# RWKV opening of a fused 1-core kernel: input loaded first, squares on two engines, key projection ahead of the low-rank products, and those in column and row groups of the array

## The chip, the cores and the metric

The kernel runs on one core of a Trainium2 chip. The metric is the device time of one launch in microseconds, lower is better. Three runs of the kernel before gave 1181.09, 1178.21 and 1175.55 us; the median is 1178.21.

## The reference, cut to what matters

Input x is 256 tokens by 1024 features, all in float32. Two blocks run one after the other: a RWKV-7 layer and a block-sparse attention layer, then an mLSTM layer and a latent-attention layer, each of these with a squared-ReLU MLP and scaled by vectors from a conditioning vector c ("ada"). The change is in the opening of the RWKV layer:

```python
h = rms_norm(x, norm_a)                     # x * rsqrt(mean(x*x) + 1e-6) * g
xx = pad(h, one step)[:, :-1] - h           # token shift
for i, wd in enumerate((1024, 64, 1024, 1024, 64, 1024)):
    outs.append((h + xx * mu[i]) @ w_in[:, off:off + wd])
r, wdn, k, v, adn, gp = outs
w = -softplus(-(w0 + tanh(wdn) @ w2)) - 0.5
a = sigmoid(a0 + adn @ a2)
kk = (k * k_k) per head, divided by its norm
k = k * (1 + (a - 1) * k_a)
# then the recurrence over time, by chunks of 64 in the kernel
```

w2 and a2 are 64 x 1024: the products wdn and adn ("lora") have 64 columns, and the products behind them ("za") contract over 64.

## The kernel before, in words

Every engine has one program written out by hand, with semaphores between them. Activations lie in `arena`, 17 pages of 128 x 2048 floats; X is page 0, XN page 13, hT page 8, xx page 7. Weights come as 95 panels of 2 MB through `ring`, a ring of four slots. SyncE's program (lines 1115 to 1131) issues x, waits until `loads` has 48 (cc, pc and pos_i, issued by ScalarE, with gn behind them), and then issues the panels in the order in which TensorE's program names them (`panel`, `ada`). Panel i goes to slot i % 4 once the last reader of panel i - 4 is through:

```python
if i >= SLOTS:
    sp.wait_ge(*order[i - SLOTS][1])
sp.dma_start(ring[:, i % SLOTS, :], stream[i]).then_inc(sem(f"slot_loaded{i % SLOTS}"), 16)
```

The opening, engine by engine:

- ScalarE: cond = Silu (L1172) once `loads` is there, a warm-up root (`warm_root`, L1220) that brings its table, both halves' squares with a sum along the row (L1214), the root x_root (L1216), then `scaled`: eight copies of the transposed input out of PSUM times norm_a (L1278). Later the sines, tanh and the plain copy of lora (L1312, L1313), sixteen sigmoids (L1316, L1317), and the copies of k (L1244).
- VectorE: `norm` refines the root (L1657 to L1663) and scales x into XN (L1676, two instructions). Then the rope angles, the difference xx over all of hT (L1802, L1803), and the mixes h + xx * mu (L1813), eight instructions for each of six products. They go to two pages in turn, so the third and fourth wait until lora is through. Behind four of them stand the partial sums of two ada panels (`ada`, L1704 and L1706), then kk (L1820), the mix of v, the scans of the decay (L1827 to L1833), the scaling of k (L1836, L1838), the mix of g, and a third ada panel. The last one waits until TensorE has summed the first ada panel's columns, which it does behind v.
- TensorE: 16 transposes of XN (L503) once both halves of XN and `loads` are there; lora (L610), two products of 128 rows by 64 columns one after the other, both out of PSUM partitions 0 to 63; once ScalarE has taken them, za (L617), eight banks with two products each, both from partitions 0 to 63; k and then r (`project_T`, L391), each two panels; sums of squares (L633), v and g (`project_tok`, L490), and between them the column sums of the ada panels (L517).

A float32 product appears in the trace as two records of load and matmul. PSUM has eight banks of 128 x 512 that `claim` hands out in turn.

## Time and profile before

| | |
|---|---|
| median of three runs | 1178.21 us |
| the profiled execution's own time | 1176.87 us |
| its span, first to last instruction | 1175.1 us |
| TensorE busy | 1093.5 us (93%) |
| VectorE busy | 741.1 us (63%) |
| ScalarE busy | 500.6 us (43%) |
| mean granted TensorE clock | 0.982 |

The busy times are sums over the whole span; the stages differ in what limits them. "L391" is line 391 of the kernel. Times in the views are microseconds from the start of the span, "ns" marks the exceptions. PE is TensorE's matmuls, PEld its weight loads, DVE VectorE, ACT ScalarE, SPq and ACTq the DMA instructions issued by SyncE and ScalarE.

### The profile page before, as it was taken

What the parts mean: (1) busy time and instruction counts of PE and PEld (TensorE: products, weight loads), DVE (VectorE), ACT (ScalarE), POOL (GpSimd) and SP (SyncE); (2) the same over time, 40 slices, a digit from 0 to 9 for tenths busy, and PEclk for the clock granted to TensorE, in tenths of its full rate; (3) what the DMA queues carried; (4) which work ended last, traced back from release to release, by engine and by line L of the source; (5) the groups of instructions that cost most, each with busy time, mean ns of one, the idle gap of its engine ahead of it and who ended that gap; (6) DMA issues with size and microseconds to landing.
All of it is one profiled execution on the core that took longest, in us unless ns stands there. A gap on an engine that the chain in (4) does not pass through costs nothing.

```text
span 1175.1 us, 19624 instructions
## 1 busy us (share of the span) xinstructions
PE 1093.5 (93%) x8492; PEld 893.6 (76%) x8492; DVE 741.1 (63%) x1145; ACT 500.6 (43%) x774; POOL 33.2 (3%) x30
## 2 busy tenths in 40 slices
PE   3999978999899997999999999999899899999997
PEld 2886458888568876777767789999757677998995
DVE  4662676855847967776557767757436566555444
ACT  3311312124444457554445555445243555554442
POOL 0000003320000010000000000000000000000000
PEclk9999989999989999999999999999999989999999
DMA  9373400430256552244534586776743534565520
GB/s 386 120 302 133 174 1 3 161 132 5 90 197 239 190 194 93 72 172 187 215 137 150 184 317 236 302 291 247 273 156 144 215 144 153 206 242 188 214 74 36
DMA packets 15078, 204.88 MB, mean 174 GB/s; under 512 B 1800, under 2 KB 1800, under 8 KB 2832
## 3 DMA queue, kind: packets, MB, share of 16 engines
q1 hardware_dynamic: 14256, 201.33, 45.4%
q10 hardware_dynamic: 736, 2.30, 0.5%
q8 instruction: 67, 1.10, 0.4%
q14 instruction: 19, 0.16, 0.0%
HBM read 202.57 MB, written 1.05 MB: 173 GB/s over the span
## 4 chain that ended last, share of the span: by engine, by line
PE 76%; DVE 15%; ACT 4%; issue 2%; DMA 2%; ACTq 0%; DVEq 0%
PE bank L432 15%; PE bank L433 15%; PE bank L434 15%; PE bank L391 6%; PE bank L688 5%; PE bank L490 5%; DVE slot_parts L1732 2%; PE bank L547 2%; DMA ring<-in_stream 1%; PE bank L517 1%; PE bank L503 1%; DVE arena L1846 1%; PE bank L670 1%; DVE small L1706 1%; PE bank L610 1%
## 5 line engine op out<-in xcount | busy, mean ns | idle before, releaser
L432 PE MATMUL bank<-page_parts 128*128 128x512 f32 (+1 forms) x1104 | 377.7, 342 | 3.9 <-DVE page_parts L1765 1.7
L1732 DVE TENSOR_TENSOR slot_parts<-ring,page_parts 128x2048 fp32r<-128x2048 f32 x104 | 237.0, 2289 | 121.2 <-ACT page_parts L1185 120.9
L1185 ACT ACTIVATE page_parts<-ring 128x2048 fp32r<-128x2048 f32 x104 | 197.7, 1910 | 140.0 <-PE bank L434 90.1
L432 PEld LDWEIGHTS bank<-page_parts 128*128 128x128 f32 x1104 | 210.1, 190 | 28.2 <-issue 3.6
L433 PE MATMUL bank<-slot_parts,page_parts 128*128 128x512 f32 x576 | 225.5, 392 | 0.0
L434 PE MATMUL bank<-page_parts 128*128 128x512 f32 x576 | 225.3, 391 | 0.0
L1244 ACT ACTIVATE arena<-bank 128x512 f32<-128x512 f32 (+1 forms) x142 | 78.7, 572 | 225.1 <-PE bank L490 66.6
L433 PE MATMUL bank<-page_parts 128*128 128x256 f32 x528 | 149.4, 283 | 0.0
L434 PE MATMUL bank<-page_parts,slot_parts 128*128 128x256 f32 x528 | 149.4, 283 | 0.0
L434 PEld LDWEIGHTS bank<-page_parts 128*128 128x128 f32 x576 | 108.8, 189 | 23.1
L433 PEld LDWEIGHTS bank<-slot_parts,page_parts 128*128 128x128 f32 x576 | 109.0, 189 | 21.6
L1706 DVE SCALAR_TENSOR_TENSOR small<-ring,small 128x512 f32<-128x512 f32 x147 | 111.2, 757 | 4.1
L433 PEld LDWEIGHTS bank<-page_parts 128*128 128x128 f32 x528 | 101.3, 192 | 0.4
L434 PEld LDWEIGHTS bank<-page_parts,slot_parts 128*128 128x128 f32 x528 | 101.2, 192 | 0.0
L490 PE MATMUL bank<-ring,arena 128*128 128x512 f32 (+2 forms) x220 | 87.8, 556 | 1.5 <-ACT arena L1278 0.8
L490 PEld LDWEIGHTS bank<-ring,arena 128*128 128x128 f32 x220 | 41.2, 190 | 44.6 <-issue 36.4
L391 PE MATMUL bank<-arena,ring 128*128 128x256 f32 x336 | 73.0, 379 | 0.0
L391 PEld LDWEIGHTS bank<-arena,ring 128*128 128x128 f32 x336 | 63.7, 190 | 8.9 <-issue 0.3
L688 PE MATMUL bank<-arena 64*64 64x64 f32 x1792 | 56.7, 224 | 3.7 <-issue 3.7
L688 PEld LDWEIGHTS bank<-arena 64*64 64x64 f32 x1792 | 55.9, 141 | 4.3 <-issue 4.1
L547 PE MATMUL bank<-ring,small 128*1 128x512 f32 x112 | 50.9, 609 | 3.4 <-DVE arena L2120 3.4
L503 PE MATMUL bank<-cc,arena 128*128 128x128 f32 x206 | 30.1, 303 | 25.2 <-DVE arena L1676 18.9
(278 smaller groups left out, 1213.3 us busy)
## 6 DMA issues: line engine op xcount, KB each, us to landing
ring<-in_stream SPq DMA_DIRECT2D x95, 2048.0 KB, 8.2
arena<-in_x SPq DMA_DIRECT2D x2, 512.0 KB, 6.6
gn<-in_gn ACTq DMA_DIRECT2D x2, 512.0 KB, 8.4
out<-arena SPq DMA_DIRECT2D x2, 512.0 KB, 2.6
cc<-in_consts ACTq DMA_DIRECT2D x1, 898.0 KB, 6.1
pc<-in_params ACTq DMA_DIRECT2D x1, 287.5 KB, 7.5
gn<-in_head_sel ACTq DMA_DIRECT2D x1, 32.0 KB
pos_i<-in_positions ACTq DMA_DIRECT2D x1, 1.0 KB, 7.3
```

Source lines behind the costliest of these rows:

```text
L391: ins = mm(b[:, half * T:(half + 1) * T], weights[:, k, ct * P:(ct + 1) * P], src[:, k, :], start=(k == 0), stop=(k == k_tiles - 1))
L432: mm(out, a[0], b[0], start=start, stop=False)
L433: mm(out, a[0], b[1], start=False, stop=False)
L434: return mm(out, a[1], b[0], start=False, stop=stop)
L490: ins = mm(b[:, 0:n], src[:, k, tb * P:(tb + 1) * P], weights[:, k, 0:n], start=(k == 0), stop=(k == k_tiles - 1))
L503: ins = nc.tensor.transpose(b[:, jj * T + tb * P:jj * T + (tb + 1) * P], src[:, tb, j * P:(j + 1) * P], ident)
L547: ins = mm(b[0:1, :], cond[:, k:k + 1], W[:, k, :], start=(k == 0), stop=(k == KT - 1))
L688: ins = mm(b[q * LC:(q + 1) * LC, j * LC:(j + 1) * LC], lhs(q, j), rhs(q, j), start=True, stop=True)
L1185: act(unit_parts(n)[0], unit_values(n)[1], ACT.Copy).then_inc(ac.step("w_hi"), 1)
L1244: act(dst, bank(product)[:, 0:n].rearrange("p (a b) -> p a b", a=dst.shape[1]) if len(dst.shape) == 3 else bank(product)[:, 0:n], kw.get(" ...
L1706: stt(part, W, cond[:, k:k + 1], part, ALU.mult, ALU.add).then_inc(dv.step("ada_part" if k == KT - 1 else "ada_sum"), 1)
L1732: tt(unit_parts(n)[1], lo, hi, ALU.subtract).then_inc(dv.step("w_lo"), 1)
```

## The change

SyncE issues x, cc, pc and then at once the panels; ScalarE issues only pos_i, and gn behind the hT copies. A one-element tile set by GpSimd lets ScalarE load the root's table at the start. ScalarE squares the first half of x and VectorE the second. VectorE makes xx and the mixes of k pair by pair as hT comes, then the mixes of w and a, which has a page of its own. TensorE does k first, with its first panel's contraction outermost; the panels' order becomes k0, k1, ada, ada, lora, r0, r1. The two lora products go to PSUM partitions 0 to 63 and 64 to 127 in turn, and za takes its two contractions from partitions 0 to 63 and 64 to 127, each with a bank of its own.

```diff
--- before.py
+++ after.py
@@ -196,7 +196,7 @@
         khat, bhat, xx, hT = page(5, KT), page(6, KT), page(7, KT), page(8, KT)
-        mix = [page(9, KT), page(10, KT)]
+        mix = {"k": page(9, KT), "w": page(10, KT), "a": page(16, KT), "r": page(10, KT), "v": page(9, KT), "g": page(10, KT)}
         LW, AA, KK, EE = page(11, KT), page(12, KT), page(13, KT), page(14, KT)
@@ -216,7 +216,7 @@
         ada_part = scratch(1024).rearrange("p (a n) -> p a n", a=2)
-        lora = arena[:, 15, 0:512].rearrange("p (a t) -> p a t", a=2)
+        lora = arena[:, 15, 0:T]
         g_scan = arena[:, 15, 512:512 + T]
@@ -246,7 +246,7 @@
         gcols = scratch(32).rearrange("p (b n) -> p b n", b=TB)
-        mid = lora
+        mid = arena[:, 15, 0:2 * T].rearrange("p (a t) -> p a t", a=2)
         newton = scratch(64).rearrange("p (a n) -> p a n", a=2)
@@ -602,29 +602,41 @@
             transposes("hT_a", XN)
+            W = wt(panel(("k", 0)), 512)
+            bs = [claim(("k", 0, i)) for i in range(2)]
+            for k in range(KT):
+                pe.wait_ge(sem("mix"), k + 1)
+                for ct in range(4):
+                    ins = mm(bs[ct // 2][:, ct % 2 * T:(ct % 2 + 1) * T], W[:, k, ct * P:(ct + 1) * P], mix["k"][:, k, :],
+                             start=(k == 0 and ct % 2 == 0), stop=(k == KT - 1), skip_group_check=True)
+                    if k == KT - 1 and ct % 2:
+                        ins.then_inc(filled(("k", 0, ct // 2)), 1)
+            panel_used()
+            project_T(("k", 1), wt(panel(("k", 1)), 512), mix["k"])
+            panel_used()
+            ada(2)
             W = panel("lora")
             b = claim("lora")
-            for a in range(2):
-                for k in range(KT):
-                    pe.wait_ge(sem("mix"), 8 * a + k + 1)
-                    ins = mm(b[0:64, a * T:(a + 1) * T], W[:, a * 512 + k * 64:a * 512 + (k + 1) * 64], mix[a][:, k, :],
+            for k in range(KT):
+                for a in range(2):
+                    pe.wait_ge(sem("mix"), 8 * (a + 1) + k + 1)
+                    ins = mm(b[a * HD:(a + 1) * HD, 0:T], W[:, a * 512 + k * HD:a * 512 + (k + 1) * HD], mix["wa"[a]][:, k, :],
                              start=(k == 0), stop=(k == KT - 1))
...
             pe.wait_ge(*evacuated("lora"))
-            for j in range(KT):
-                b = claim(("za", j))
-                for a in range(2):
-                    ins = mm(b[:, a * T:(a + 1) * T], W[0:64, 1024 + a * D + j * P:1024 + a * D + (j + 1) * P],
-                             lora[0:64, a, :], start=True, stop=True)
-                ins.then_inc(filled(("za", j)), 1)
+            for i in range(4):
+                bs = [claim(("za", i, a)) for a in range(2)]
+                for jj in range(2):
+                    j = 2 * i + jj
+                    for a in range(2):
+                        r = slice(a * HD, (a + 1) * HD)
+                        ins = mm(bs[a][:, jj * T:(jj + 1) * T], W[r, 1024 + j * P:1024 + (j + 1) * P], lora[r, :], start=True, stop=True)
+                        if jj:
+                            ins.then_inc(filled(("za", i, a)), 1)
             panel_used()
-            for n, name in ((2, "k"), (3, "r")):
-                for half in range(2):
-                    project_T((name, half), wt(panel((name, half)), 512), mix[n % 2],
-                              wait=("mix", 8 * n) if half == 0 else None)
-                    panel_used()
-                if name == "k":
-                    ada(2)
+            for half in range(2):
+                project_T(("r", half), wt(panel(("r", half)), 512), mix["r"], wait=("mix", 24) if half == 0 else None)
+                panel_used()
@@ -634,7 +646,7 @@
                 for half in range(2):
-                    project_tok((name, half), wt(panel((name, half)), 512), mix[n % 2],
+                    project_tok((name, half), wt(panel((name, half)), 512), mix[name],
                                 wait=("mix", 8 * n) if half == 0 else None)
@@ -1116,8 +1128,8 @@
                 sp.dma_start(X[:, tb, :], x[0, tb * P:(tb + 1) * P, :]).then_inc(sem(f"x_loaded{tb}"), 16)
-            sp.wait_ge(sem("loads"), 48)
+            sp.dma_start(cc[:, :], cc_d).then_inc(sem("loads"), 16)
+            sp.dma_start(pc[:, :], pc_d).then_inc(sem("loads"), 16)
             for i, (name, released) in enumerate(order):
@@ -1131,6 +1143,7 @@
         def _(pool):
+            nc.gpsimd.memset(root_warm, 1.0).then_inc(sem("warm"), 1)
             level = con("level").rearrange("p (l t) -> p l t", l=6)
@@ -1163,13 +1176,9 @@
-            act_.dma_start(cc[:, :], cc_d).then_inc(sem("loads"), 16)
-            act_.dma_start(pc[:, :], pc_d).then_inc(sem("loads"), 16)
             act_.dma_start(pos_i[:, :], pos_d).then_inc(sem("loads"), 16)
-            for a in range(2):
-                act_.dma_start(gn[:, a, :], gn_d[a:a + 1, :].to_broadcast([P, D])).then_inc(sem("gn_rows"), 16)
-            act_.wait_ge(sem("loads"), 48)
-            act(cond, par("cond"), ACT.Silu).then_inc(ac.step("cond"), 1)
+            act_.wait_ge(sem("warm"), 1)
+            act(root_warm, root_warm, ACT.Sqrt).then_inc(ac.step(), 1)
@@ -1203,9 +1212,7 @@
                 for tb in range(TB):
-                    if branch == "x":
-                        act_.wait_ge(sem(f"x_loaded{tb}"), 16)
-                    elif branch:
+                    if branch:
                         for half in range(2):
@@ -1302,22 +1309,32 @@
-            warm_root()
-            x_squares("x")
+            act_.wait_ge(sem("x_loaded0"), 16)
+            act(XN[:, 0, :], X[:, 0, :], ACT.Square, accum_out=x_sq[:, 0:1]).then_inc(ac.step("x_sq"), 1)
+            act_.wait_ge(*ac.last)
+            act_.wait_ge(sem("x_sq_late"), 1)
+            act_.wait_ge(sem("loads"), 48)
+            act(x_root, x_sq, ACT.Sqrt, scale=1.0 / D, bias=con("eps")).then_inc(ac.step("x_root"), 1)
             scaled("hT_a", hT, par("norm_a"))
+            act(cond, par("cond"), ACT.Silu).then_inc(ac.step("cond"), 1)
+            for a in range(2):
+                act_.dma_start(gn[:, a, :], gn_d[a:a + 1, :].to_broadcast([P, D])).then_inc(sem("gn_rows"), 16)
             act_.wait_ge(sem("angles"), 1)
...
                 act(rope2[:, a], rope2[:, a], ACT.Sin).then_inc(ac.step("tables"), 1)
-            act_.wait_ge(*finished("lora"))
-            act(lora[0:64, 0, :], bank("lora")[0:64, 0:T], ACT.Tanh).then_inc(ac.step(), 1)
-            act(lora[0:64, 1, :], bank("lora")[0:64, T:2 * T], ACT.Copy).then_inc(ac.frees("lora"), 1)
-            for j in range(KT):
-                act_.wait_ge(*finished(("za", j)))
-                act(LW[:, j, :], bank(("za", j))[:, 0:T], ACT.Sigmoid, bias=par("w0")[:, j:j + 1]).then_inc(ac.step("sig"), 1)
-                act(AA[:, j, :], bank(("za", j))[:, T:2 * T], ACT.Sigmoid, bias=par("a0")[:, j:j + 1]).then_inc(ac.frees(("za", j)), 1)
             for half in range(2):
...
                     copy(khat[:, 4 * half + 2 * i:4 * half + 2 * i + 2, :], ("k", half, i))
+            act_.wait_ge(*finished("lora"))
+            act(lora[0:HD, :], bank("lora")[0:HD, 0:T], ACT.Tanh).then_inc(ac.step(), 1)
+            act(lora[HD:P, :], bank("lora")[HD:P, 0:T], ACT.Copy).then_inc(ac.frees("lora"), 1)
+            for i in range(4):
+                for a, (dst, base) in enumerate(((LW, "w0"), (AA, "a0"))):
+                    act_.wait_ge(*finished(("za", i, a)))
+                    for jj in range(2):
+                        j = 2 * i + jj
+                        act(dst[:, j, :], bank(("za", i, a))[:, jj * T:(jj + 1) * T], ACT.Sigmoid, bias=par(base)[:, j:j + 1]).then_inc(
+                            ac.frees(("za", i, a)) if jj else ac.step(), 1)
             for h in range(2):
@@ -1667,10 +1684,10 @@
-                norms[0] += TB
-                dve.wait_ge(sem("x_sq"), norms[0])
+                norms[0] += 1
+                dve.wait_ge(sem("x_sq"), TB * norms[0] - 1)
                 ts(ss, x_sq, 1.0 / D, EPS, ALU.mult, ALU.add).then_inc(dv.step(), 1)
-                dve.wait_ge(sem("x_root"), norms[0] // TB)
+                dve.wait_ge(sem("x_root"), norms[0])
                 refined(ss, x_root, ss)
@@ -1766,11 +1783,38 @@
-            for tb in range(TB):
-                dve.wait_ge(sem(f"x_loaded{tb}"), 16)
+            dve.wait_ge(sem("x_loaded1"), 16)
+            V.tensor_tensor_reduce(XN[:, 1, :], X[:, 1, :], X[:, 1, :], 1.0, 0.0, ALU.mult, ALU.add,
+                                   accum_out=x_sq[:, 1:2]).then_inc(dv.step("x_sq_late"), 1)
+            dve.wait_ge(*dv.last)
+            dve.wait_ge(sem("x_loaded0"), 16)
             norm()
             dve.wait_ge(sem("loads"), 48)
-            dve.wait_ge(sem("cond"), 1)
+            mix_waits = {"r": "lora", "v": ("k", 1, 1), "g": ("r", 1, 1)}
+            def mixed(name, which, j):
+                mu = par("mu")[:, 8 * which:8 * which + 8]
+                stt(mix[name][:, j, :], xx[:, j, :], mu[:, j:j + 1], hT[:, j, :], ALU.mult, ALU.add).then_inc(dv.step("mix"), 1)
+            def mixes(name, which):
+                if name in mix_waits:
+                    dve.wait_ge(*finished(mix_waits[name]))
+                for j in range(KT):
+                    mixed(name, which, j)
+            for i in range(4):
+                s = slice(2 * i, 2 * i + 2)
+                dve.wait_ge(*evacuated(("hT_a", i)))
+                tt(xx[:, s, 1:T], hT[:, s, 0:T - 1], hT[:, s, 1:T], ALU.subtract).then_inc(dv.step(), 1)
+                ts(xx[:, s, 0:1], hT[:, s, 0:1], -1.0, None, ALU.mult).then_inc(dv.step(), 1)
+                dve.wait_ge(*dv.last)
+                for j in (2 * i, 2 * i + 1):
+                    mixed("k", 2, j)
+            mixes("w", 1)
+            mixes("a", 4)
             ts(one_m_ka, par("ka"), -1.0, 1.0, ALU.mult, ALU.add).then_inc(dv.step(), 1)
@@ -1798,28 +1842,15 @@
             ts(rope2[:, 0], rope2[:, 0], float(np.pi / 2), None, ALU.add).then_inc(dv.step("angles"), 1)
-            dve.wait_ge(*evacuated(("hT_a", 3)))
-            tt(xx[:, :, 1:T], hT[:, :, 0:T - 1], hT[:, :, 1:T], ALU.subtract).then_inc(dv.step(), 1)
-            ts(xx[:, :, 0:1], hT[:, :, 0:1], -1.0, None, ALU.mult).then_inc(dv.step(), 1)
-            dve.wait_ge(*dv.last)
-            last_use = {2: "lora", 3: "lora", 4: ("k", 1, 1), 5: ("r", 1, 1)}
-            def mixes(n, which):
-                if n in last_use:
-                    dve.wait_ge(*finished(last_use[n]))
-                mu = par("mu")[:, 8 * which:8 * which + 8]
-                for j in range(KT):
-                    stt(mix[n % 2][:, j, :], xx[:, j, :], mu[:, j:j + 1], hT[:, j, :], ALU.mult, ALU.add).then_inc(dv.step("mix"), 1)
-            for n, which in enumerate((1, 4, 2, 0)):
-                mixes(n, which)
+            dve.wait_ge(sem("cond"), 1)
             ada(2 * KT)
...
                 ts(KK[:, j, :], khat[:, j, :], par("kk")[:, j:j + 1], None, ALU.mult).then_inc(dv.step("kkr"), 1)
-            mixes(4, 3)
-            dve.wait_ge(*evacuated(("za", 7)))
+            mixes("r", 0)
+            mixes("v", 3)
+            for a in range(2):
+                dve.wait_ge(*evacuated(("za", 3, a)))
             scan = g_scan.rearrange("p (c t) -> p c t", c=NC_)
@@ -1836,7 +1867,7 @@
                 tt(khat[:, j, :], khat[:, j, :], mid[:, j % 2, :], ALU.mult).then_inc(dv.step(), 1)
-            mixes(5, 5)
+            mixes("g", 5)
             ada(KT)
@@ -2323,7 +2354,7 @@
             out[i, :, 0:512], out[i, :, 512:1024] = tiles(wa[:, 1024:1088]), tiles(wa[:, 3136:3200])
-            out[i, 0:64, 1024:2048], out[i, 0:64, 2048:3072] = w["w2_a"][0], w["a2_a"][0]
+            out[i, 0:64, 1024:2048], out[i, 64:128, 1024:2048] = w["w2_a"][0], w["a2_a"][0]
         elif name in (("q2",), ("k2",)):
...
```

## Rows read from the trace of the kernel before

**Rows 1.** The page: the span, and part 4, the chain by engine.

```profile
span 1175.1 us, 19624 instructions
...
PE 76%; DVE 15%; ACT 4%; issue 2%; DMA 2%; ACTq 0%; DVEq 0%
```

**Rows 2.** The chain of waits, 0 to 240 us: start us, us, what.

```profile
1.66 7.35 DMA pos_i<-in_positions
...
12.87 0.30 ACT small L1216
...
15.55 1.10 PE bank L503 x4
...
20.11 2.28 DVE arena L1802
...
23.14 9.44 PE bank L610 x32
...
33.30 7.17 PE bank L617 x32
40.47 55.45 PE bank L391 x256
...
173.06 13.03 PE bank L670 x256
```

**Rows 3.** VectorE's timeline at 127 us; in brackets the idle time before it and its releaser.

```profile
127.77 0.49 DVE L1704 TENSOR_SCALAR small<-ring,small 128x512 f32<-128x512 f32 x1 [28.55 <-PE bank L517]
128.29 0.75 DVE L1706 SCALAR_TENSOR_TENSOR small<-ring,small 128x512 f32<-128x512 f32 x1
```

**Rows 4.** ScalarE, line L1214 (squares of x): ns min/median/max, first and last start.

```profile
L1214 ACT ACTIVATE arena<-arena x2: 1038/1038/1039, 10.7 to 11.7; 128x1024 f32<-128x1024 f32 x2
```

**Rows 5.** The page, part 6: DMA issues, KB each, us to landing.

```profile
arena<-in_x SPq DMA_DIRECT2D x2, 512.0 KB, 6.6
...
cc<-in_consts ACTq DMA_DIRECT2D x1, 898.0 KB, 6.1
pc<-in_params ACTq DMA_DIRECT2D x1, 287.5 KB, 7.5
```

**Rows 6.** Windows: busy us (x instructions) of PE, PEld, DVE, ACT, POOL; PEclk, DMA share, GB/s.

```profile
0.00:8.20 8.20, 0.00 (x0) 0.00 (x0) 0.00 (x0) 1.28 (x1) 0.21 (x4) 1.00 0.74 281
```

**Rows 7.** SP, L1125 (weight panels), issued at 9 to 11 and 54 to 55 us.

```profile
L1125 SPq DMA_DIRECT2D ring<-in_stream x4: 328/432/532, 9.0 to 10.3; - x4
...
DMA to landing us min/median/max: 7.9/14.5/21.1
...
L1125 SPq DMA_DIRECT2D ring<-in_stream x1: 328/328/328, 54.5 to 54.5; - x1
...
DMA to landing us min/median/max: 8.4/8.4/8.4
```

**Rows 8.** VectorE, lines L1906 (product's nearest size) and L1827 (scan).

```profile
L1906 DVE TENSOR_TENSOR arena<-arena,gn x2: 1215/1216/1216, 250.8 to 252.0; 128x1024 f32<-128x1024 f32 x2
...
L1827 DVE TENSOR_TENSOR_SCAN arena<-cc,arena x8: 690/691/693, 72.9 to 84.9; 128x256 f32<-128x256 f32 x8
```

**Rows 9.** Timelines of ScalarE and VectorE, 16 to 30 us.

```profile
16.67 3.40 ACT L1278 ACTIVATE arena<-bank,pc 128x256 f32<-128x256 f32 x8 [3.51 <-PE bank L503]
...
22.51 6.42 DVE L1813 SCALAR_TENSOR_TENSOR arena<-arena,pc 128x256 f32<-128x256 f32 x16
```

**Rows 10.** Windows, columns as in rows 6.

```profile
23.10:27.80 4.70, 4.66 (x11) 2.60 (x12) 4.70 (x13) 0.00 (x0) 0.00 (x0) 1.00 1.01 432
27.90:32.60 4.70, 4.67 (x22) 2.71 (x20) 1.03 (x3) 0.00 (x0) 0.00 (x0) 1.00 0.51 220
167.50:171.00 3.50, 3.41 (x16) 3.42 (x17) 0.13 (x2) 1.75 (x3) 0.00 (x0) 0.50 0.00 0
```

**Rows 11.** TensorE, line L610: ns min/median/max of a record.

```profile
L610 PEld LDWEIGHTS bank<-arena,ring x32: 137/137/231, 23.1 to 32.0; 128*64 128x64 f32 x32
L610 PE MATMUL bank<-arena,ring x32: 379/379/660, 23.1 to 32.2; 128*64 128x256 f32 x32
```

## The prediction

> **What bounds the kernel now.** I read the page first: the chain that ended last lies for 76% on TensorE [rows 1]: the kernel is bound by one engine in most stages, and what a change is worth must be read from the stage it touches. The diff touches only the first 130 us, so the next view is the chain of waits in order of time for that stretch [rows 2]. It has three pieces. Up to 12.87 us it waits for loads (the last to land is pos_i, at 9.0) and then for ScalarE's squares and root. From 15.55 to 127.77 it is TensorE: transposes, the low-rank opening (L610 and L617), then 55.45 us of L391, which is the key projection and the receptance projection, 27.73 each, so r starts at 40.47 + 27.73 = 68.20. From 127.77 on it is VectorE. The third view, VectorE's timeline, shows how the second piece hands over to the third: VectorE had idled 28.55 us when the matmuls of L517 (the column sums that stand behind v in TensorE's program) let it go on [rows 3]. So what TensorE gains before r starts moves the start of r, and with it 127.77 and all that follows, by the same time. From r's start to 127.77 are 59.57 us, and the diff leaves that work alone.
>
> **Head: x loaded first, squares on two engines.** Before, x_root started at 12.87: loads down at 9.0, then a Silu, a table load, a warm-up root and two squares one after the other [rows 2, 4]. After, the table load and the warm-up need no load, cond's Silu stands behind the hT copies, and the squares of the two halves run side by side, so x_root waits for whichever is later, the squares or `loads`. The loads: x, cc and pc are 2 x 0.524 + 0.920 + 0.294 = 2.26 MB [rows 5]. In the trace 281 GB/s x 8.2 us = 2.30 MB had moved by 8.2 us [rows 6], and nothing now comes ahead of these: 8.1 us is the lower end. The upper end comes from the queue's own pace: four panels issued at 9.0 to 10.3 landed 7.9 to 21.1 us after their issue, 4.8 us from one to the next, which is 2.10 MB / 4.8 = 437 GB/s and leaves 7.9 - 4.8 = 3.1 us that are fixed [rows 7]: 0.74 + 3.1 + 2.26/0.437 = 9.0 us. I take 8.6. The squares: x's halves land at about 5.0 and 6.2 by the same rule; ScalarE's takes 1.04 [rows 4] and the reading of its sum, to 6.2. VectorE's multiply with a sum over 128x1024 isn't in the trace; it lies between a plain product of that size (1.22) and the pace of the scan (0.69 for 256, so 2.8) [rows 8]; I take 1.2, being a product, and get 7.4. Even 2.8 ends at 9.0, 0.4 us behind the loads. x_root at 8.65 instead of 12.87 gains **4.2 us** (3.8 to 4.7). The short chain from there to the transposes (2.68 us) stays: they start at T = 11.3 instead of 15.55.
>
> **Key projection first.** Before, from 15.55 to r's start are 52.65 us: 3.65 transposes, 3.94 idle until the first mix, 9.44 for L610, 0.7 for its evacuation, 7.17 for L617, 27.73 for k [rows 2]. The 3.94 idle are the copies of all four pairs (3.40), then 2.28 of difference over all of hT, then a mix [rows 9]. After, VectorE follows pair by pair: it can start 0.85 + 1.1 us after T, and a pair costs 2.28/4 for its difference, 0.2 for the first column and 2 x 0.40 for two mixes [rows 2, 9], 1.6 us. The first mix is ready at T + 3.2, before the transposes end at T + 3.65, and two rows of k cost TensorE 16 records of 0.213 us = 3.4 us, twice what VectorE needs: the idle time goes. Its cover is that factor of two. k's panel, first behind the inputs, lands at 0.74 + 3.1 + 4.36/0.437 = 13.8 us, and is wanted at 15.0; this edit has 1.2 us of slack. k then costs 27.73.
>
> The clock: from 23.1 to 27.8 TensorE did 11 records in 4.7 us and from 27.9 on 22 in the same time, though the column of the granted clock says 1.00 in both; at 167.5 to 171 the column says 0.50, the 1.2 GHz level, after VectorE had held TensorE up [rows 10]. So TensorE starts slow after an idle stretch, and before it paid this twice, for transposes and for L610. After, it has no gap between transposes and k. If the full rate comes 4.75 us after work begins, as behind 23.1, only 1.1 us of k is slow, which loses **0.6 us** (none to 2.4, should it count from k's start again). k ends at T + 32.0 = 43.3.
>
> **Low-rank products side by side, and what is late next.** One record of 128x256 takes 0.213 us when they follow each other [rows 10], so the 32 of lora are 6.8 us; the 32 of za took 7.17. The trace has no matmul with 128 rows and 64 columns next to its neighbour, nor a pair in two row groups with 128 columns. The nearest row is L670: 256 records of 64x64 with 128 columns in 13.03 us, 0.051 each [rows 2], where the same pace per column (0.213/2) would be 0.107. Its pairs go to the two column groups in turn, as lora's will. So they halve: 3.4 and 3.6; the other end is no overlap, 6.8 and 7.2. With the evacuation between them, 3.4 + 0.7 + 3.6 = 7.7 us lie between k's end and r.
>
> But another thing is now later. Slots are freed in the panels' order, and that order is now k0, k1, ada, ada, lora, r0: r0 takes the second slot, which k's second half frees at 43.3 (before, k's first half freed it, 14 us ahead of r's need). r0's before was issued at 54.5, 0.2 us after k's first half ended (40.47 + 13.86), and landed 8.4 us later; the first of the four at 9.0 took 7.9 [rows 7]. So a panel lands 8.1 to 8.6 us after the end that frees it. I take **8.4 us**, 0.7 more than the products need: TensorE waits for the panel, and the overlap of the products can give no more than this. r1 and v0 queue behind r0 and land in order 4.8 us apart, while r0 alone works 13.9 us. lora's own panel is freed by k0 at about 29.4 and lands near 38: hidden behind k1, with 5 us to spare.
>
> A rule on this: the Trainium skill, TensorE: Matmul & The Clock Gate, section Measured speedup vs the span model, gives 3.07x for four row tiles and 2.38x for three column tiles. An estimate by that page's shares of the ideal (0.77 and 0.79) would make the two products 4.7 and 4.3, with evacuation 9.7, and the whole gain 15.1 us instead of 16.4; L670's row shows the full factor of two, and no run here shows its row-tile case.
>
> The other engines. ScalarE: copies of k, then tanh, then 16 sigmoids at 0.43 us [rows 9], about 7 us and a table load behind lora, so to about 56; r's first banks are free after two of them. VectorE, which now does the angles and two ada panels (8 products of up to 0.75 us each [rows 3], 6 us a panel) behind the mixes of k, w and a, is free near 41, and r's eight mixes (3.2 us) wait for lora's end at 46.7: ready by 50 for r at 51.7. Its scans behind za and g's mixes, which wait for r, end near 83, well before the 111 at which v's sums come. gn's two loads, now behind cond, have over 100 us until they are read. All these cost nothing as long as r waits for its panel.
>
> **Sum.** r starts at T + 3.65 + 27.73 + 0.6 + 8.4 = T + 40.4 instead of T + 52.65: 12.25. With the head's 4.2: **16.4 us** less. The profiled execution took 1176.87 (span 1175.10 and 1.77 around it), 1.3 below the median 1178.21. It becomes 1160.5, the median 1161.8.
>
> **Rivals.**
> *The packed products overlap in part or not.* With no overlap 6.8 + 0.7 + 7.2 = 14.7 us follow k instead of 8.4: gain 10.1, time 1168.1. With only za serial 11.3: gain 13.5, 1164.7. For it: the trace shows no overlap with all 128 rows in use, where two streams must be fed at full width. Against it: L670's 0.051 us.
> *Slower: each change of tile empties the array.* Then every one of the 64 records would cost its own length and load, 0.38 + 0.14 as in L610 [rows 11]: 33.3 us, with evacuation 34.0, against 8.4: 25.6 lost, 16.4 gained, 1187.4. It decides from 0.377 us a record up. L670 changes its tile at every pair and shows 0.051.
> In the Trainium skill, TensorEngine Tiling (Array Packing), section Key Properties, a change of the tiling mode drains TensorE, a change of tile doesn't; the modes change equally often before and after, so by it this rival fails.
> *No change: the loads don't go in order.* If SP's first eight transfers shared the engines evenly, cc would be down only after 6.0 MB (17.5 us) and k's panel after all 10.65 MB, 0.74 + 3.1 + 24.4 = 28.2 us. k would start there instead of at 15.0, gain 16.4 - 13.2 = 3.2 us: 1175. For it: before, SP waited for `loads` ahead of the first panel. Against it: the four panels issued together landed one after the other, 7.9 to 21.1 us [rows 7].
>
> **Chances.** The forecast 0.64: its own range is 1159 to 1165. Overlap in part or none 0.22. Loads out of order 0.03. The emptying array 0.03, and 0.02 for a loss as large that I don't see. The remaining 0.06 are small losses that leave over 6 us of gain. A difference below 0.5% (5.9 us) can hardly be told from none with this kernel. So faster 0.92, same 0.03, slower 0.05. The range: below, head 4.7, no slow clock, panel after 8.1, which is 17.8, and the 2.7 us by which a run before fell under its median: 1158. Above, both products serial, 1168.1, and most of the bounds on the clock: 1169.5.
>
> **What would show it.** x_root near 8.6 and transposes at 11.3 (a transpose at 15 refutes the head). k's first matmul 3.6 us after the first transpose. lora's 32 records in 3.4 us and za's in 3.6 (near 7 each: the first rival). A wait of 0.7 us for ring ahead of r, and r near 51.7. Then VectorE idle until about 111.3. I would be wrong above all if r0's panel came later than 8.4 us after k, or if k were starved of mixes or of its panel.

## The result, and the profile after

The changed kernel took 1163.07 us in the median of four runs (1159.56 to 1164.23), the kernel before 1176.99 in the median of its four (1175.55 to 1181.09). Set against each other the ratio is 0.9864, interval 0.9843 to 0.9885: 13.5 to 18.5 us less, 16.0 in the middle. The two medians by themselves lie 13.9 us apart, inside that interval; wherever this text gives a gain by time, it is the one by the ratio. I had forecast 1161.8 us, 1158 to 1169.5, from a gain of 16.4. The profiled execution took 1164.23, the longest of the four; its span is 1162.4.

The chain of waits of the changed kernel (start us, us, what), which answers to [rows 2]. L610 is now k's first panel, L623 lora, L633 za, L391 k's second panel and then r:

```profile
2.10 6.88 DMA pc<-in_params
...
9.10 0.30 ACT small L1317
...
11.78 3.65 PE bank L503 x16
15.43 14.38 PE bank L610 x64
29.81 13.81 PE bank L391 x64
43.63 3.63 PE bank L623 x32
...
48.11 3.72 PE bank L633 x32
51.84 27.82 PE bank L391 x128
...
110.58 0.91 PE bank L517 x8
```

The reader sees TensorE without a gap from 11.78 to 43.63, then 0.85 us for ScalarE to empty lora's bank (43.63 + 3.63 to 48.11), za, and r at 51.84 instead of 68.20. lora's 32 records take 3.63 us and za's 3.72, against 9.44 and 7.17 before. VectorE's timeline, which answers to [rows 3] and shows the new square as well:

```profile
6.07 1.22 DVE L1787 CUSTOM_DVE_ANT_0 arena<-arena 128x1024 f32<-128x1024 f32 x1 [6.07 <-DMA arena<-in_x]
...
111.51 0.48 DVE L1721 TENSOR_SCALAR small<-ring,small 128x512 f32<-128x512 f32 x1 [28.55 <-PE bank L517]
```

VectorE is let go at 111.51 instead of 127.77: 16.26 us earlier. The 28.55 us of idle time ahead of it are the same to the hundredth, since both ends hang on r. The transfer of r's first panel, issued when k ended, to be held against [rows 7]:

```profile
L1137 SPq DMA_DIRECT2D ring<-in_stream x1: 328/328/328, 43.7 to 43.7; - x1
...
DMA to landing us min/median/max: 7.9/7.9/7.9
```

It landed at 51.6, 0.2 us before za was through.

So the opening gave 16.3 us, and yet this execution's span is only 12.7 us shorter. I followed the difference between the same instructions in both traces along the span. On VectorE's instructions it is -16.3 at the release, between -14.5 and -17.0 up to 570 us of the kernel before, and falls from -15.5 to -12.8 between 572 and 577 us; from there on it stays between -11.8 and -12.8, and at the end it is -12.6. There the kernel runs heads of the mLSTM layer, which the diff does not touch. A window at that place, before and then after (columns as in [rows 6]):

```profile
570.00:580.00 10.00, 8.67 (x37) 6.26 (x38) 4.16 (x9) 1.22 (x4) 0.00 (x0) 1.00 0.92 390
```

```profile
554.50:564.50 10.00, 8.64 (x25) 6.31 (x26) 3.74 (x9) 0.72 (x3) 0.00 (x0) 0.66 0.92 392
```

The granted clock is 1.00 before and 0.66 after, and TensorE starts 25 matmul records in those 10 us against 37, busy for the same 8.7 us. Whether that belongs to the change is what the first experiment asks.

### The profile page after: what moved, and what is told of

It is laid out like the page before. It is cut to its first block, busy times and chain, and to the rows that moved or that the text cites. A ratio compares the mean times of both kernels' runs of the same rounds, so it can differ in the third digit from the quotient of the medians.

```text
span 1162.4 us, 19633 instructions
## 1 busy us (share of the span) xinstructions
PE 1085.8 (93%) x8492; PEld 888.6 (76%) x8492; DVE 743.5 (64%) x1153; ACT 495.9 (43%) x770; POOL 33.7 (3%) x31
## 4 chain that ended last, share of the span: by engine, by line
PE 76%; DVE 15%; ACT 3%; issue 2%; DMA 2%; SPq 0%; DVEq 0%; ACTq 0%
PE bank L432 15%; PE bank L434 15%; PE bank L433 15%; PE bank L391 5%; PE bank L700 5%; PE bank L490 5%; DVE slot_parts L1749 2%; PE bank L547 2%; DMA ring<-in_stream 1%; PE bank L503 1%; PE bank L517 1%; PE bank L610 1%; DVE arena L1877 1%; PE bank L682 1%; DVE small L1723 1%
## 5 line engine op out<-in xcount | busy, mean ns | idle before, releaser
L391 PE MATMUL bank<-arena,ring 128*128 128x256 f32 x272 | 59.3, 379 | 0.0
L700 PE MATMUL bank<-arena 64*64 64x64 f32 x1792 | 53.8, 218 | 5.5 <-issue 5.5
L700 PEld LDWEIGHTS bank<-arena 64*64 64x64 f32 x1792 | 53.1, 135 | 6.0 <-issue 5.8
L391 PEld LDWEIGHTS bank<-arena,ring 128*128 128x128 f32 x272 | 51.5, 190 | 7.3 <-DMA ring<-in_stream 0.3
```

The source lines that it names most:

```text
L391: ins = mm(b[:, half * T:(half + 1) * T], weights[:, k, ct * P:(ct + 1) * P], src[:, k, :], start=(k == 0), stop=(k == k_tiles - 1))
L700: ins = mm(b[q * LC:(q + 1) * LC, j * LC:(j + 1) * LC], lhs(q, j), rhs(q, j), start=True, stop=True)
```

## The experiments

Each variant starts from the changed kernel unless it says otherwise. The table has the marks that the profiles share: r's start, VectorE's release, and where it was timed in several rounds the gain that the ratio against the kernel before gives with its interval.

| kernel | r starts | VectorE released | gain by time, us |
|---|---|---|---|
| before | 68.20 | 127.77 | |
| changed, first profile | 51.84 | 111.51 | 16.0 (13.5 to 18.5) |
| changed, again | 51.34 | 111.02 | 15.7 (13.3 to 18.0) |
| head_only | 63.58 | 123.15 | 4.0 (2.0 to 6.0) |
| low_first | 60.05 | 119.76 | 8.8 (5.5 to 12.0) |
| k_inner | 53.45 | 113.12 | 13.3 (10.5 to 16.3) |
| serial | 63.13 | 125.02 | 7.3 (5.0 to 9.8) |
| serial, second profile | 58.96 | 118.64 | |
| lora_serial | 53.74 | 113.41 | |
| za_serial | 54.13 | 113.80 | |
| za_narrow | 52.00 | 114.70 | |
| early_root | 50.91 | 110.66 | 16.1 (13.1 to 19.2) |
| lora_between | 49.45 | 109.12 | 17.1 (14.1 to 20.0) |

**The changed kernel again.** No edit.

> The changed kernel once more, unaltered. Theory: the opening is set by waits and durations that repeat, so x_root stands at 9.1, r starts at 51.8 and VectorE is let go at 111.5 as in the first profile; the 2.8 us that the first profile gave back between 572 and 577 us of the kernel before belong to that execution's clock, so they need not stand in this one, and the timed gain is about 16 us. Rival: they are a consequence of the change, as a different phase of transfers and of TensorE's gaps in that stage; then every profile of it shows the shift fall from 15.7 to 12.8 us there, and the timed gain is about 13 us.

VectorE's timeline, and the window at the place where the first profile had lost:

```profile
111.02 0.49 DVE L1721 TENSOR_SCALAR small<-ring,small 128x512 f32<-128x512 f32 x1 [28.55 <-PE bank L517]
...
555.00:560.00 5.00, 4.57 (x20) 3.41 (x21) 1.50 (x6) 0.53 (x1) 0.00 (x0) 1.00 1.01 429
```

Released at 111.02, and the granted clock is 1.00 at the place in question. The difference to the kernel before stays between -14.9 and -18.3 us up to the end of the span, where it is -16.3. So the rival as I put it, that every profile shows the loss, falls.

But the place isn't one execution's accident either. The variants below pass the same point of the program, and in head_only, which changes nothing but the head, its window reads:

```profile
570.10:573.60 3.50, 3.50 (x10) 2.76 (x10) 0.00 (x0) 0.49 (x1) 0.00 (x0) 0.50 1.01 431
```

Of the twelve profiles with a changed opening seven lose 1.6 to 2.9 us against the kernel before between 572 and 577 us of it, with a granted clock of 0.50 to 0.61 there: the first of the changed kernel, head_only, the second of serial, lora_serial, za_serial, early_root and lora_between. The other five, and the one profile of the kernel before, stand at 1.00. What decides it isn't known, and one profile of the kernel before can't tell whether it falls there too in some executions. The timed gains of 16.0 and 15.7 us lie near the 16.3 and 16.8 at the release, but with intervals of some 2.5 us to either side they don't exclude a mean loss of one or two.

**The head alone**, on the kernel before:

```diff
-            sp.wait_ge(sem("loads"), 48)          # SyncE; cc, pc and gn no longer from ScalarE at the start
+            sp.dma_start(cc[:, :], cc_d).then_inc(sem("loads"), 16)
+            sp.dma_start(pc[:, :], pc_d).then_inc(sem("loads"), 16)
...
-            warm_root()
-            x_squares("x")
+            act(XN[:, 0, :], X[:, 0, :], ACT.Square, accum_out=x_sq[:, 0:1]).then_inc(ac.step("x_sq"), 1)
...
+            V.tensor_tensor_reduce(XN[:, 1, :], X[:, 1, :], X[:, 1, :], 1.0, 0.0, ALU.mult, ALU.add,
+                                   accum_out=x_sq[:, 1:2]).then_inc(dv.step("x_sq_late"), 1)
```

> The kernel before with the head alone: x, cc and pc issued by SyncE with the panels behind, gn later, root table early, squares on two engines; everything from the transposes on as before. Theory: x_root at 9.1 instead of 12.87, and that is passed on whole: r starts at 64.4, VectorE is let go at 124.0, 3.8 us faster (1173.5 us). Rival: the earlier start is lost again, because TensorE's full clock comes at the same time of day or because lora's panel now lands behind cc, and r stays within 1 us of 68.2.

Chain of waits and VectorE's timeline; here L610 is lora as before:

```profile
9.17 0.30 ACT small L1307
...
19.45 8.51 PE bank L610 x32
...
123.15 0.49 DVE L1708 TENSOR_SCALAR small<-ring,small 128x512 f32<-128x512 f32 x1 [28.56 <-PE bank L517]
```

x_root stands at 9.17, 3.7 us earlier, and it is passed on whole: transposes 3.7 earlier. The release is even 4.6 earlier, since L610 took 8.51 us instead of 9.44. Two windows of it:

```profile
19.40:23.40 4.00, 3.95 (x12) 2.36 (x13) 4.00 (x11) 0.00 (x0) 0.00 (x0) 0.64 1.05 445
23.40:28.00 4.60, 4.55 (x22) 2.60 (x19) 1.86 (x6) 0.02 (x1) 0.00 (x0) 1.00 1.00 419
```

12 records in the first 4 us and 22 in the next 4.6: the half pace, here with 0.64 in the clock's column, ended sooner behind L610's start than in [rows 10], where the first 4.7 us held 11. The rival falls.

What the head owes to which of its edits, no run separates, but ScalarE's timeline in the changed kernel speaks against a gain from the squares on two engines:

```profile
9.10 0.30 ACT L1317 ACTIVATE small<-small,cc 128x2 f32<-128x2 f32 x1 [3.34 <-DMA pc<-in_params]
```

It was free from 5.76 us on, and x's second half was there when VectorE began on it at 6.07. ScalarE's square of the first half, with the reading of its sum, took 1.15 us; by that, an estimate, it would have had the second one at 7.2, no later than VectorE, and pc landed at 8.98 anyway.

**Low-rank products ahead of k**, with the mixes of w and a pair by pair, and ScalarE's program in the same order:

```diff
             transposes("hT_a", XN)
+            W = panel("lora")     # lora and za here, packed, k and then r behind them
...
                 for j in (2 * i, 2 * i + 1):
-                    mixed("k", 2, j)
-            mixes("w", 1)
-            mixes("a", 4)
+                    mixed("w", 1, j)
+                    mixed("a", 4, j)
+            mixes("k", 2)
```

> The changed kernel with the low-rank products ahead of the key projection: mixes of w and a pair by pair, then k's; lora, za, k, r in TensorE's program; still packed. Theory: TensorE then follows VectorE through the 16 mixes, lora ends at 23.8, za at about 28.3, k at 56.0, and r starts there without a wait for its panel, 4.2 us later than with k ahead; 1167 us. Rival: the order gives nothing of its own, as it only trades the idle time ahead of lora for the wait for r's panel, and r starts at 51.8 to 52.8.

```profile
25.00 5.41 PE bank L620 x32
30.40 14.01 PE bank L629 x64
44.41 13.83 PE bank L391 x64
...
58.89 0.61 DVE arena L1849 x2
59.51 0.41 DVE arena L1799
...
60.05 27.86 PE bank L391 x128
```

```profile
25.00:30.40 5.40, 5.40 (x33) 4.29 (x33) 4.09 (x17) 4.51 (x10) 0.00 (x0) 0.68 0.96 406
```

lora ends at 24.14 and the mixes pace it, as expected. r starts 8.2 us later than with k ahead, not 4.2. The additional 4.0 have four parts: lora ended 0.3 late; za took 5.41 us instead of 3.72 under a clock of 0.68; k's two panels took 0.2 us over their 27.6; and 1.8 us lie in the variant itself, as the chain shows: r's mix (L1799 at 59.51) stands behind kk's last two products (L1849), which wait for k's end. Without those 1.8 the order by itself is worth 6.4 us here, and 4.7 where the slow stretch does not fall on za. Whether that stretch belongs to this order isn't shown: lora at the mixes' pace had kept TensorE busy for only 5.4 of the 9.9 us ahead of za, but there is one profile. By time the two kernels are 6.9 us apart (15.7 and 8.8).

**k's contraction innermost again:**

```diff
-            W = wt(panel(("k", 0)), 512)
-            bs = [claim(("k", 0, i)) for i in range(2)]
-            for k in range(KT):
-                pe.wait_ge(sem("mix"), k + 1)
...
+            project_T(("k", 0), wt(panel(("k", 0)), 512), mix["k"], wait=("mix", 0))
```

> The changed kernel with k's first panel as all others: column tile by column tile, the contraction innermost, each step of it waiting for its mix. Theory: the first column tile needs all eight mixes, and the last is ready at about 20.3; k's first panel then ends at 20.3 + 0.4 + 7 x 3.46 = 45 - 0.1 less what overlapped, that is k ends near 45.1 instead of 43.4, and part of it at the slow clock, so r starts 1.5 to 3 us later (53.3 to 54.8) and VectorE is let go near 113.5. Rival: the mixes come faster than TensorE reads, so contraction outermost gives nothing and r stays within 0.5 us of 51.6.

```profile
19.40 0.49 DVE arena L1791
...
19.93 25.30 PE bank L391 x116
45.24 3.63 PE bank L615 x32
```

The chain now runs through VectorE's mixes up to 19.89, and k ends at 45.24, where 45.1 was expected. r starts 1.6 to 2.1 us later. Contraction outermost is worth that much.

**Both low-rank products one after the other:**

```diff
-            for k in range(KT):
-                for a in range(2):
+            for a in range(2):
+                for k in range(KT):
...
-                    ins = mm(b[a * HD:(a + 1) * HD, 0:T], W[:, a * 512 + k * HD:...], mix["wa"[a]][:, k, :],
+                    ins = mm(b[0:HD, a * T:(a + 1) * T], W[:, a * 512 + k * HD:...], mix["wa"[a]][:, k, :],
...
-                        ins = mm(bs[a][:, jj * T:(jj + 1) * T], W[r, 1024 + j * P:...], lora[r, :], start=True, stop=True)
+                        ins = mm(bs[a][:, jj * T:(jj + 1) * T], W[0:HD, 1024 + a * D + j * P:...], lora[0:HD, a, :], start=True, stop=True)
```

> The changed kernel with the low-rank products as before: both lora products to partitions 0 to 63, one after the other, both za products from partitions 0 to 63. Theory: lora takes 6.9 us and za 7.2 instead of 3.6 and 3.7, r no longer waits for its panel and starts at 58.4 instead of 51.8, VectorE is let go at 118.1, and 9.6 us of gain against the kernel before stay (1167 us). Rival: the gain of the packing is small because other waits stand behind it, so that less than 2 us go.

```profile
43.69 7.07 PE bank L623 x32
...
51.47 11.66 PE bank L632 x32
63.13 30.03 PE bank L391 x128
...
55.00:60.00 5.00, 5.00 (x14) 3.89 (x13) 2.20 (x6) 2.76 (x7) 0.00 (x0) 0.50 0.99 426
```

lora's 7.07 us were expected (6.9), za's 11.66 and r's 30.03 for 27.8 were not: the clock fell to 0.50 inside za. That could be an execution's own accident or the work of a half-used array, so I profiled the kernel a second time, and with it two variants that change nothing but the order of one loop nest.

> The kernel with both low-rank products one after the other, profiled again. Theory: the fall of the granted clock to 0.50 inside za belongs to that execution, as the ones elsewhere; here za takes 7.2 us and VectorE is let go at 118 to 119. Rival: the unpacked products bring it about, and it stands here again at the same place, with VectorE let go near 125.

```profile
44.01 7.07 PE bank L623 x32
...
51.79 7.17 PE bank L632 x32
58.96 27.82 PE bank L391 x128
...
118.64 0.48 DVE L1720 TENSOR_SCALAR small<-ring,small 128x512 f32<-128x512 f32 x1 [28.55 <-PE bank L517]
```

za 7.17, release at 118.64 as expected: the fall doesn't belong to every execution of this kernel. Without it the packing is worth 58.96 - 51.84 = 7.1 us.

**One of the two unpacked, by the order alone.** za_serial claims all its eight banks first, which the cut leaves out:

```diff
-            for k in range(KT):        # lora_serial: loops swapped
-                for a in range(2):
+            for a in range(2):
+                for k in range(KT):
...
-                for jj in range(2):    # za_serial: all eight tiles of one row group, then of the other
-                    for a in range(2):
+            for a in range(2):
+                for j in range(KT):
```

> The changed kernel with lora's two loops swapped: all eight steps of w into the lower 64 columns of the array, then all eight of a into the upper, so that neighbours share their column group; nothing else differs. Theory: the packing lies in the order alone; lora takes 6.9 us instead of 3.6, its panel wait ahead of r goes, and r starts 3.1 to 3.4 us later, 54.7 to 55.1. Rival: two column groups with all 128 rows in use overlap however they are ordered, or r's panel hides the difference, and r starts by 52.

```profile
42.90 6.26 PE bank L623 x32
...
53.74 27.82 PE bank L391 x128
```

> The changed kernel with za's products ordered by row group: eight from partitions 0 to 63, then eight from 64 to 127; nothing else differs. Theory: as with lora, 7.2 us instead of 3.7, r 3.3 to 3.5 us later, 54.8 to 55.2, if TensorE keeps its full clock. Rival: half of the array idle lets the clock fall to its lower level, as in the profile of both products one after the other (11.66 us); then za takes 9 us or more here too.

```profile
47.74 6.39 PE bank L631 x32
54.13 27.82 PE bank L391 x128
```

r starts 1.9 to 2.4 and 2.3 to 2.8 us later, where I expected at least 3. That neighbours must lie in different groups is shown: 6.26 against 3.63 us, and 6.39 against 3.72. The rival of za_serial, a low clock from a half-used array, didn't show: the clock stayed at 1.00.

But neither reaches the 7.07 and 7.17 of the serial layout, though within each half all records share their group. The traces show where the 0.8 us go. Windows of lora_serial, inside the first half and at the seam (columns as in [rows 6]):

```profile
44.00:45.00 1.00, 1.00 (x6) 0.65 (x5) 0.18 (x1) 0.00 (x0) 0.00 (x0) 1.00 0.79 164
45.40:46.40 1.00, 1.00 (x11) 0.73 (x9) 0.00 (x0) 0.00 (x0) 0.00 (x0) 1.00 0.89 377
```

The records start 0.216 us apart in both halves, but the seven starts behind the 13th take 0.71 us together instead of 1.51 (za_serial: 0.76). Around the seam the last records of one group and the first of the other overlap as they do in the packed order, and nowhere else.

**za cut to 16 columns:**

```diff
-                        ins = mm(bs[a][:, jj * T:(jj + 1) * T], ..., lora[r, :], start=True, stop=True)
+                        ins = mm(bs[a][:, jj * T:jj * T + 16], ..., lora[r, 0:16], start=True, stop=True)
```

> The changed kernel with each za product cut to 16 of its 256 columns; this leaves out 240 of the 256 tokens of w and a. Theory: r starts when its panel has landed, 8.2 us after k's end, whatever za costs, so za's end moves from 51.8 to about 48.8 and r's start stays at 51.3 to 51.8, behind a wait for ring of some 2.5 us. Rival: the packed products set r's start and the panel is there already; then r starts near 48.5.

TensorE's timeline, then the chain of waits:

```profile
48.41 1.96 PE L633 MATMUL bank<-arena,ring 64*128 64x16 f32 x32 [0.88 <-ACT arena L1330]
...
43.96 8.00 DMA ring<-in_stream
...
52.00 30.85 PE bank L391 x128
```

za is through at 50.4, 1.4 us sooner, and r still starts at 52.00, 8.04 us after k's end, behind the transfer. That r cannot start sooner than its panel is shown. za's end missed the expected 48.8, and so the wait was 1.6 us and not 2.5: with a sixteenth of the columns its 32 records still took 1.96 us, 0.061 each, for 3.72 before. r itself then took 30.85 us, part of it at a clock of 0.50, behind 4.5 us in which TensorE had been busy for 1.96; that is why the release is late.

**A version with smaller first loads:**

```diff
-            sp.dma_start(cc[:, :], cc_d).then_inc(sem("loads"), 16)
+            sp.dma_start(cc[:, 0:P], cc_d[:, 0:P]).then_inc(sem("ident_loaded"), 16)
-            sp.dma_start(pc[:, :], pc_d).then_inc(sem("loads"), 16)
+            sp.dma_start(pc[:, :], pc_d).then_inc(sem("params_loaded"), 16)
             for i, (name, released) in enumerate(order):
+                if i == 1:
+                    sp.dma_start(cc[:, P:NCONST], cc_d[:, P:NCONST]).then_inc(sem("loads"), 16)
...
-            act_.wait_ge(sem("loads"), 48)
-            act(x_root, x_sq, ACT.Sqrt, scale=1.0 / D, bias=con("eps")).then_inc(ac.step("x_root"), 1)
+            act(x_root, x_sq, ACT.Sqrt, scale=1.0 / D, bias=root_eps).then_inc(ac.step("x_root"), 1)
```

> The changed kernel with smaller first loads: the root's bias from a tile that GpSimd sets, cc in two transfers, its first 128 columns (the identity) behind x, then pc, then k's first panel, then the rest of cc. Theory: x_root is freed by the squares at 7.4 instead of by pc at 9.1; nothing else on the way to r is late, and every step moves 1.7 us: transposes at 10.1, r at 49.9, VectorE let go at 109.7, about 17.5 us faster than the kernel before. Rival: pc or the identity, now the last before the transposes and hT, or k's panel lands later than the root needs, and less than 0.7 us is left.

```profile
7.29 0.30 ACT small L1321
...
9.96 3.65 PE bank L504 x16
13.61 15.20 PE bank L611 x64
...
42.66 8.21 DMA ring<-in_stream
...
13.60:18.00 4.40, 4.40 (x16) 3.72 (x16) 4.29 (x12) 2.37 (x5) 0.00 (x0) 1.00 0.99 424
```

The root came at 7.29 and the transposes at 9.96, 1.8 us sooner, as expected. At r 0.4 to 0.9 us of it are left and at the release the same: k's first panel took 15.20 us against 14.38 and 13.94, with 16 records in the first 4.4 us (0.275 us each). That is nearly the number of the rival, but not by its reason: no load was late. The earlier start was spent at the slow pace. Whether it brought that about isn't settled: in the seven profiles whose transposes start at 11.5 to 11.8 us and that do k in this way, k's first panel took 13.94 to 14.87 us, in the two that start them near 9.9 it took 15.20 and 14.68. By time this version can't be told from the changed kernel.

**And with lora between k's two panels:**

```diff
             panel_used()
+            W = panel("lora")          # its sixteen products; r's panel then takes k's first slot
...
             project_T(("k", 1), wt(panel(("k", 1)), 512), mix["k"])
             panel_used()
-            ada(2)
+            ada(1)                     # the other one behind r
             pe.wait_ge(*evacuated("lora"))
```

> early_root with lora's product between k's two panels, za behind k, the panels in the order k0, lora, k1, ada, r0, r1, ada, v0, and the second ada panel summed later on VectorE. Theory: ScalarE empties lora's bank while TensorE works on k's second panel, which takes 0.85 us out of the path, and r's panel takes the slot of k's first and is there long before, so r starts 0.9 to 1.0 us earlier than in early_root, at about 49.0, VectorE is let go at 108.7. Rival: the second ada panel, now behind r's panels and on VectorE behind the mix of g, makes VectorE the one that is late at v's end, and the 28.5 us wait shrinks to nothing with the end later than 109.7.

```profile
31.79 14.01 PE bank L392 x64
45.80 3.65 PE bank L635 x32
49.45 27.82 PE bank L392 x128
...
109.12 0.48 DVE L1729 TENSOR_SCALAR small<-ring,small 128x512 f32<-128x512 f32 x1 [22.45 <-PE bank L518]
```

za follows k at once and r follows za at once: r starts 1.5 us before early_root (0.5 of it in k's first panel, 14.68 us here) and 1.9 to 2.4 before the changed kernel, the release comes at 109.12. VectorE's idle time ahead of it shrank by 6.1 us, the one ada panel, and is far from gone: the rival falls. The median of four is 1160.49 us, ratio 0.9855 (0.9830 to 0.9880). It is the best opening by the profile, but the intervals of this and of the changed kernel overlap for the most part.

## Why the prediction was right

Point by point, with the first profile of the changed kernel.

- **What the gain hangs on.** That r's start passes whole to VectorE's release and further: 59.57 us lie between the two before, 59.67 after, and the difference stayed until the end in the second profile. Right.
- **The loads** came at the upper end of the bracket, not in its middle. pc landed at 8.98; by the queue's pace it should be down at 9.0. x_root stood at 9.10 instead of 8.65, and the head gave 3.77 us for 4.2. The term was 0.43 us too large.
- **The squares**: VectorE's took 1.22 us, started at 6.07 and was through at 7.3, as taken from the plain product. That the second engine wasn't needed for it, the prediction didn't see.
- **Key first**: k's first matmul stood 3.65 us after the first transpose, as forecast, and TensorE had no gap in k. k_inner shows that this needs the contraction outermost.
- **The clock**: k's first panel took 14.38 and its second 13.81, so 0.57 us were lost for a forecast of 0.6. The next profile lost 0.13, the second of serial 1.06 and early_root 1.4; that the first profile met the number is luck, it is one draw out of a spread, as the range of none to 2.4 had it.
- **Packing**: 3.63 and 3.72 us for 3.4 and 3.6. The first rival, no overlap or half of it, is refuted for both products; so is the emptying array. That is 1.95 and 1.93 times the pace of one group alone (7.07 and 7.17 us). The Trainium skill, TensorE: Matmul & The Clock Gate, section Measured speedup vs the span model, gives 2.38x for three column tiles and 3.07x for four row tiles. The estimate from these shares, 1.58 and 1.54 for two tiles, was too low here, and the measurement decides.
- **r's panel**: here a balance came out differently. I expected 7.7 us of products and evacuation and a wait of 0.7 for the panel. It was 3.63 + 0.85 + 3.72 = 8.2 us, and the panel landed 0.2 us before the end: the wait that I had put last wasn't there. The sum is the same within 0.2, as r started 8.2 us after k for a forecast of 8.4, because two errors of 0.4 to 0.5 us balanced; za_narrow shows the panel as the floor 0.2 us below the products.
- **Loads in order**: pc landed before any panel did. That rival is refuted.

Together: head 3.77 for 4.2, then 52.65 - 40.06 = 12.59 us for 12.25, and 16.3 for 16.4 at the release. The mechanism stood as forecast; that the sum came within 0.1 us is luck, since the head was too large and the rest too small. By parts: 3.7 for the head, from head_only; packing 7.1, from serial; and what is left, about 5.5, for k first with VectorE following by pairs, of which the contraction outermost is 1.6 to 2.1. The 5.5 are a remainder; low_first puts them at 4.7 to 6.4.

By time the two comparisons give 16.0 and 15.7. What the prediction did not say is how much one execution can differ from the next by the clock: the first profile showed a gain of 12.7 us over its span and the second one of 16.3, with the same opening but for 0.5 us.

## What to carry to other kernels

Where one engine feeds another at a fixed distance, mark that release in both traces and judge an edit of the opening there; the span adds every later turn of the clock to it. A slot ring turns a change of order into a change of deadlines: write down for each panel who frees its slot and when it is wanted, because a panel that is freed at the last moment sets a floor (here 8.0 us) under which faster work gives nothing. Small products overlap where neighbours in program order lie in different row or column groups; with one group's products all ahead of the other's only the seam gains, here 0.8 us of 3.4.

## What the runs showed of the hardware that I had not expected

- Two column groups with all 128 rows in use overlap (32 records in 3.63 us for 7.07), and so do two row groups with all 128 columns (3.72 for 7.17). The trace of before had shown neither.
- With the two groups in separate halves of the order the same work took 6.26 and 6.39 us, 0.8 less than with one group only: the records overlap around the seam of the halves. The 14th record of lora_serial to start takes 430 ns, as elsewhere only the first of a group does (the others take 379). If it is the first of the second half, it started ahead of three that stand before it in the program.
- 32 records of 64 rows, 128 columns of weights and 16 moving columns took 1.96 us, 0.061 each, for 3.72 with 256 moving columns.
- The granted clock fell to 0.50 in the middle of dense float32 work in one execution of serial (za 11.66 us) and not in the next (7.17). At one point of the mLSTM stage, 573 us in the kernel before, it stood at 0.50 to 0.61 in seven of thirteen profiles and at 1.00 in the others. An earlier start of TensorE can be lost to a slow stretch: of early_root's 1.8 us, 0.9 were left at the release against the first profile and 0.4 against the second.
